# Side-by-side high and low activations in the 256-token feed-forwards of a two-block transformer kernel

## Chip, cores and metric

One core of one Trainium2 chip runs the whole program. The metric is the device time of one execution in microseconds (us). The kernel's text names the engines `tensor` (TensorE, PE in the profile), `vector` (VectorE, DVE), `scalar` (ScalarE, ACT), `gpsimd` (GpSimd, POOL) and `sync` (SyncE, SP, which only starts transfers).

## The reference, cut to what matters

Four transformer layers of width 1024 run over 256 tokens; the first of them also carries 256 context tokens, so its matrices meet 512 tokens. Layers 1 and 2 have one feed-forward each, layers 3 and 4 have two each. That makes six feed-forwards, of which five see 256 tokens:

```python
D_FF = 2816
def swiglu(h, w_in, w_out):            # first two layers; swiglu_2 is the same with silu(g) * u
    a, u = jnp.split(h @ w_in, 2, axis=-1)
    return (jax.nn.silu(a) * u) @ w_out
# layer 2:        x = x + g2 * swiglu(modulate(rms_norm(x, norm2), sh2, sc2), w_ffn_in, w_ffn_out)
# layers 3 and 4: x = x + 0.5 * swiglu_2(rmsnorm(x, g), w_gu, w_down)   before and after the mixer
```

## The kernel before

**Layout.** Features lie on the 128 partitions, tokens along the free dimension (`S` = 256, `SQ` = 512). The 1024 features are 8 chunks (`KC`), the 2816 hidden features 22 tiles (`FT`).

**Products.** A product in full precision is made of three matmuls of float32r parts. Weights and activations are each split into a high part (a rounding copy) and a low part (the value less its high part); `product` (line 873) adds high x high, high weight x low activation and low weight x high activation into one PSUM tile. So each output tile takes three weight loads and three matmuls of 256 columns for each of its chunks. PSUM tiles of these products take three banks in turn (`LIN`), and a tile waits in `room` until the tile three before it has been read.

**Weights.** A "piece" is one transfer into a ring of four slots. ScalarE copies its two halves to `w_hi` (line 1205), of which there are two; VectorE subtracts, half by half, into `ring_lo` (line 1608), in the same place as the piece. Both do this in `ahead`, at the head of their work for an item: at item i they split the piece of item i+1, and ScalarE may begin once TensorE has begun item i's own piece (line 1202), since only then the other `w_hi` is free.

**A feed-forward** (`ffn`, line 659) has 22 `gate_up` items and 8 `resid` items; each engine goes through the items in this one order. A `gate_up` item has one piece of 2048 columns (gate and up weights of one hidden tile): TensorE makes the gate tile a and then the up tile u, 24 matmuls each. In the feed-forwards of layers 3 and 4 ("scaled") the norm's factor `row` is applied behind the product. The order on the other engines at item i is

- ScalarE: split of the next piece; `hid_part` (line 1303, high part of the hidden tile i-1); silu of a (line 1315 if scaled, else line 1318 straight from PSUM).
- VectorE: split of the next piece; `hid_rest` (line 1730, low part of the hidden tile i-1); if scaled, a times `row` out of PSUM (line 1743); the multiply of silu(a) by u (line 1750).
- GpSimd: nothing.

The buffers `tmp` (in `prob_t`) alternate, 512 wide each, of which 256 are in use here. A `resid` item has two pieces of 1408 columns, 11 hidden tiles each, and one output tile; VectorE adds it to the residual (lines 1772 and 1774 if scaled, line 1780 else), ScalarE makes the next stage's high part and a square (lines 1218 and 1222), GpSimd adds the squares (line 1499), VectorE makes the low part (line 1787). Output tile 0 goes chunk by chunk through the three matmuls, waiting for each hidden tile in turn; the others take all matmuls with the high weights of a piece first and those with the low weights last.

Of the kernel before, what the change touches and what calls it, by code (L numbers as in the profile page):

```python
# [122 lines left out]
class Fill:  # L123


    def __init__(self, bank, room, full, taken):
        self.bank, self.room, self.full, self.taken = bank, room, full, taken

# [52 lines left out]
def hybrid_kernel(nc, xt, vec_d, con_d, tables_d, rpb, w, out):  # L181

    with ExitStack() as ctx:  # L183
# [11 lines left out]
        h_hi = sb("h_hi", KC * SQ, F32R)  # L195
        l_at = nc.sbuf_base
        h_lo = sb("h_lo", KC * SQ, F32R)
# [24 lines left out]
        hid_hi, hid_lo = over("hid_hi", FT * S, a_at), over("hid_lo", FT * S, a_at + 4 * FT * S)  # L222
# [17 lines left out]
        gate_lo = over("gates_b", KC * S, h_at + 4 * KC * S, F32)  # L240
        gate_hi = over("gates_c", KC * S, l_at + 4 * KC * S, F32)
# [32 lines left out]
        def plain(a):  # L274
            return a.bitcast(F32)

        def v(name, at=0, n=1):
            return vec[:, VEC[name] + at:VEC[name] + at + n]
# [17 lines left out]
        silu_done, hid_hi_ready, hid_ready = sem("silu_done"), sem("hidden_hi_ready"), sem("hidden_ready")  # L296
        two_in, two_out, gains_ready = sem("two_norms_in"), sem("two_norms_out"), sem("gains_ready")
# [112 lines left out]
        def gate_up(src, i, T, fresh=None, norm=None, scaled=False):  # L410
# [4 lines left out]
            u = linear()  # L415
            if norm:
                norm.update(spread(**norm["of"]))
            add("gate_up", p=p, i=i, T=T, a=a, u=u, fresh=fresh, norm=norm, n=count("hid"), late=i > 0, scaled=scaled,
                silu=count("silu") if scaled else None, prev=last_u[0])
            last_u[0] = u  # L420

        def resid(srcs, tiles, T, how, parts, g=None, nxt=None):

            pieces, tiles = [piece(s, n) for s, n in srcs], [(c, linear()) for c in tiles]
            xd = [count("x_done") if how == "half" else None for _ in tiles]
# [58 lines left out]
        def first_block(l):  # L484
# [152 lines left out]
            for u in range(4):  # L637
                resid([(w["wo"][l][u], SLOT)], (2 * u, 2 * u + 1), T, "mod",
                      [[(0, (k * 2 + m) * P, k) for k in range(KC)] for m in range(2)], (l, 16), ("stats",))
                plan.items[-1].update(src=(h_hi, h_lo, SQ, "mg", plan.counts["mg"] - KC))  # L640
# [7 lines left out]
            for half in range(2):  # L648
# [5 lines left out]
                for c in range(KC):  # L654
                    resid([(down[2 * c + half], 11 * P)], (c,), T, "mod", [[(0, k * P, k) for k in range(11)]], (l, 40),
                          ("stats",) if half else None)
                    plan.items[-1].update(src=(hid_hi, hid_lo, T, "hid", plan.counts["hid"] - FT // 2))

        def ffn(w_in, w_out, how, g, nxt, fresh=None, norm=None):
# [5 lines left out]
            for c in range(KC):  # L665
                resid([(w_out[2 * c + k], 11 * P) for k in range(2)], (c,), S, how,
                      [[(k // 11, (k % 11) * P, k) for k in range(FT)]], g, nxt)
                plan.items[-1].update(src=(hid_hi, hid_lo, S, "hid", plan.counts["hid"] - FT))
# [4 lines left out]
        def second_block(l):  # L673
# [140 lines left out]
            for u in range(4):  # L814
                resid([(w["out2"][l][u], SLOT)], (2 * u, 2 * u + 1), S, "plain",
                      [[(0, (k * 2 + m) * P, k) for k in range(KC)] for m in range(2)], None, ("defer", v("g_ffn2", 8 * l, 8)))
                plan.items[-1].update(src=(mg2_hi, mg2_lo, S, "mg", plan.counts["mg"] - KC))
# [36 lines left out]
        def _(pe):  # L854
# [18 lines left out]
            def product(fs, n, groups, fresh=None, need=None):  # L873
# [5 lines left out]
                left = [3 * sum(len(terms) for _, terms in groups)] * len(fs)  # L879
# [1255 lines left out]
```

## Time and profile before

| what | value |
|---|---|
| time, median of 3 runs | 2614.39 us (2610.23 to 2614.93) |
| span of the profiled execution, first to last instruction | 2610.7 us |
| TensorE busy | 2504.7 us, 96% |
| VectorE busy | 1348.3 us, 52% |
| ScalarE busy | 1147.7 us, 44% |
| GpSimd busy | 343.9 us, 13% |
| granted TensorE clock, mean | 0.986 |

The profile gives the span of its execution; what the device time holds beyond it is not shown, and the span lies 3.7 us under the median. Busy shares are averages over the whole program. In the timelines a row is an instruction, or several alike merged with their count; the bracket behind it is how long the engine had been idle and what ended that.

### The profile page before, as it was taken

The page shows a single profiled execution, that of the slowest core. Times are in us where ns is not written, and L with a number is a line of the kernel's source. Part 1 is how long each engine was busy: PE and PEld are TensorE (multiplying, and loading weights), DVE is VectorE, ACT ScalarE, POOL GpSimd, SP SyncE. Part 2 cuts the span into 40 slices and gives each one's busy share as a digit, 9 for nine tenths or more (in the row PEclk, how much of TensorE's full clock was granted, in tenths as well). Part 3 has the DMA queues.
Part 4 walks back from the last instruction along what each step waited for, and adds up shares of the span by engine and source line. Part 5 has one row for each costly group of instructions (what it writes and reads, how often), then busy time and mean ns, then how long its engine had stood idle before and what let it go on. Part 6 is the DMA issues. An engine that isn't in the chain of part 4 may idle for free. (4 is left out here: it accounts for less than half of the span.)

```text
span 2610.7 us, 40864 instructions
## 1 busy us (share of the span) xinstructions
PE 2504.7 (96%) x17090; PEld 2211.8 (85%) x17090; DVE 1348.3 (52%) x2303; ACT 1147.7 (44%) x1966; POOL 343.9 (13%) x340
## 2 busy tenths in 40 slices
PE   6998999999999999999999999989999999998998
PEld 3754778677777877899999998989999998898998
DVE  2235335433323535655566567556556566656554
ACT  4243443422222525554454444555445444445443
POOL 1233312000001205200000000230000000023000
PEclk9998999999999999999999999999999999999999
DMA  8523123353443322345455443345455454334544
GB/s 295 211 72 111 65 81 129 132 177 122 147 163 131 138 81 82 130 160 180 167 210 185 170 168 118 132 151 179 169 188 193 163 188 148 126 116 167 179 169 139
DMA packets 70424, 393.43 MB, mean 151 GB/s; under 512 B 6688, under 2 KB 6848, under 8 KB 39904
## 3 DMA queue, kind: packets, MB, share of 16 engines
q1 hardware_dynamic: 60864, 350.89, 39.0%
q0 software_dynamic: 9376, 39.91, 4.3%
q8 instruction: 136, 2.23, 0.3%
q14 instruction: 48, 0.39, 0.1%
HBM read 389.73 MB, written 1.05 MB: 150 GB/s over the span
## 5 line engine op out<-in xcount | busy, mean ns | idle before, releaser
L897 PE MATMUL ps<-h_hi,w_hi 128*128 128x256 f32 (+1 forms) x3424 | 957.7, 311 | 15.4 <-ACT h_hi L1253 13.7
L1608 DVE TENSOR_TENSOR ring_lo<-ring,w_hi 128x1024 fp32r<-128x1024 f32 (+3 forms) x712 | 770.8, 1124 | 378.1 <-ACT w_hi L1205 377.9
L897 PE MATMUL ps<-h_lo,w_hi 128*128 128x256 f32 (+1 forms) x3424 | 942.6, 307 | 0.0
L1205 ACT ACTIVATE w_hi<-ring 128x1024 fp32r<-128x1024 f32 (+3 forms) x712 | 642.9, 951 | 459.1 <-PE ps L897 415.8
L897 PEld LDWEIGHTS ps<-h_hi,w_hi 128*128 128x128 f32 x3424 | 654.8, 192 | 71.6 <-issue 42.4
L897 PEld LDWEIGHTS ps<-h_lo,w_hi 128*128 128x128 f32 x3424 | 655.0, 192 | 28.4
L897 PE MATMUL ps<-h_hi,ring_lo 128*128 128x256 f32 (+1 forms) x3424 | 573.2, 306 | 0.0
L897 PEld LDWEIGHTS ps<-h_hi,ring_lo 128*128 128x128 f32 x3424 | 490.5, 192 | 28.8
L897 PE MATMUL ps<-hid_hi,w_hi 128*128 128x256 f32 (+1 forms) x1056 | 287.6, 301 | 0.0
L897 PE MATMUL ps<-hid_lo,w_hi 128*128 128x256 f32 (+1 forms) x1056 | 287.2, 301 | 0.0
L1533 POOL TENSOR_SCALAR logits<-logits,stat 128x512 f32<-128x512 f32 (+2 forms) x140 | 161.4, 1166 | 614.9 <-DVE stat L1856 614.9
L1750 DVE TENSOR_TENSOR prob_t<-prob_t,ps 128x256 f32<-128x256 f32 (+1 forms) x132 | 61.5, 466 | 309.0 <-issue 279.0
L1499 POOL TENSOR_TENSOR logits<-logits 128x256 f32<-128x256 f32 (+1 forms) x77 | 72.5, 941 | 1087.5 <-ACT logits L1222 895.8
L897 PEld LDWEIGHTS ps<-hid_hi,w_hi 128*128 128x128 f32 x1056 | 202.0, 191 | 8.5 <-issue 1.7
L897 PEld LDWEIGHTS ps<-hid_lo,w_hi 128*128 128x128 f32 x1056 | 202.0, 191 | 6.9
L897 PE MATMUL ps<-hid_hi,ring_lo 128*128 128x256 f32 (+1 forms) x1056 | 180.7, 301 | 0.0
L1357 ACT ACTIVATE logits<-logits,stat 128x512 f32<-128x512 f32 (+2 forms) x140 | 81.5, 583 | 186.9 <-DVE logits L1844 87.6
L897 PEld LDWEIGHTS ps<-hid_hi,ring_lo 128*128 128x128 f32 x1056 | 151.6, 191 | 6.8
L1315 ACT ACTIVATE prob_t<-prob_t 128x256 f32<-128x256 f32 x88 | 36.7, 418 | 161.5 <-DVE prob_t L1743 161.5
L1222 ACT ACTIVATE logits<-x_res 128x256 f32<-128x256 f32 (+1 forms) x88 | 40.8, 466 | 124.1 <-DVE x_res L1780 85.0
L897 PE MATMUL ps<-y_lo,w_hi 128*128 128x256 f32 (+1 forms) x272 | 77.6, 307 | 0.0
L1780 DVE SCALAR_TENSOR_TENSOR x_res<-ps,mod,x_res 128x256 f32<-128x256 f32 x64 | 28.6, 480 | 93.5 <-PE ps L897 93.5
(240 smaller groups left out, 2280.4 us busy)
## 6 DMA issues: line engine op xcount, KB each, us to landing
ring<-w_ffn_in SPq DMA_DIRECT2D x132, 1024.0 KB, 4.9
ring<-w_ffn_out SPq DMA_DIRECT2D x96, 704.0 KB, 4.1
ring<-w_in SPq DMA_DIRECT2D x42, 1024.0 KB, 4.9
ring<-w_w_in SPq DMA_DIRECT2D x30, 1024.0 KB, 4.9
bias_t<-w_mod POOLq DMA_DIRECT2D x24, 1024.0 KB, 8.1
ring<-w_mod SPq DMA_DIRECT2D x16, 1024.0 KB, 6.0
ring<-w_up SPq DMA_DIRECT2D x16, 576.0 KB, 3.7
ring<-w_pab SPq DMA_DIRECT2D x8, 1024.0 KB, 4.8
```

The costliest lines, as they stand in the source:

```text
L897: mm = pe.matmul(ps[fs[k].bank][:, 0:n], (hi_w if wpart == "hi" else lo_w)[0:rows, at[k]:at[k] + P], hi if part == "hi" else lo, start=lef ...
L1205: act.activation(w_hi[q.s % 2][:, h * n:(h + 1) * n], ring[q.slot][:, h * n:(h + 1) * n], ACT.Copy)\
L1222: act.activation(by_s(dst, T), xt_of(c, T), ACT.Square).then_inc(squares, 1)
L1315: act.activation(t, t, ACT.Silu).then_inc(silu_done, 1)
L1357: act.activation(lg, lg, ACT.Exp, scale=-1.0, bias=stat[:, o:o + 1], accum_out=stat[:, 4 + o:5 + o])\
L1499: pool.tensor_tensor(sq_sum[:, 0:n], sq_sum[:, 0:n], sq[c % 2][:, 0:n], ALU.add).then_inc(sq_added, 1)
L1533: pool.tensor_scalar(lg, lg, stat[:, 8 + (a % 2) * 2 + h:9 + (a % 2) * 2 + h], None, ALU.mult)\
L1608: dve.tensor_tensor(ring_lo[q.slot][:, c], ring[q.slot][:, c], plain(w_hi[q.s % 2][:, c]), ALU.subtract)\
L1750: dve.tensor_tensor(tmp[2 + i % 2][:, 0:T], t, ps[u.bank][:, 0:T], ALU.mult).then_inc(psum_taken[u.bank], 1)
L1780: ins = dve.scalar_tensor_tensor(xs(c, s), ps[f.bank][:, s * S:(s + 1) * S], mod[l][:, o:o + 1], xs(c, s), ALU.mult, ALU.add)
```

## The change

In the feed-forwards of 256 tokens the high and low parts of the activations lie side by side, 512 columns wide (`h_all`, `hid_all`). The high weights meet both in one matmul of 512 columns ("both"), whose two halves of a PSUM bank then hold the product with the high and with the low part; the low weights meet the high part in one matmul of 256, added to the first half. So a chunk takes two weight loads and two matmuls in place of three. The two halves have to be added:

- `gate_up`: VectorE takes all 512 columns of a out of PSUM (times `row`, or a plain copy in layer 2), GpSimd adds the halves, ScalarE takes silu in SBUF. VectorE multiplies the 512 columns of u by silu(a) used twice, GpSimd adds the halves, and only then can `hid_part` begin.
- `resid`: VectorE adds the halves to the residual in two instructions, with a wait for the first between them.

In products by chunk, the first chunk takes "both" first; the others take the low weights first. All else, the 512-token layer too, keeps its order.

```diff
@@ product (TensorE)
-                left = [3 * sum(len(terms) for _, terms in groups)] * len(fs)
+                two = fs[0].two
+                left = [(2 if two else 3) * sum(len(terms) for _, terms in groups)] * len(fs)
...
+                    if two and by_chunk:
+                        order = [(*parts, t, k) for i, t in enumerate(terms)
+                                 for parts in ((("lo", "hi"), ("hi", "both")) if i or left[0] < first else (("hi", "both"), ("lo", "hi")))
+                                 for k in range(len(fs))]
+                    elif two:
+                        order = [("hi", "both", t, 0) for t in terms] + [("lo", "hi", t, 0) for t in terms]
@@ ScalarE
-            def hid_part(u, i, T):
-                taken(u)
-                act.activation(at_T(hid_hi, i, T), tmp[2 + i % 2][:, 0:T], ACT.Copy).then_inc(hid_hi_ready, 1)
+            def hid_part(g, i, T):
+                if g["u"].two:
+                    act.wait_ge(halves_summed, g["summed"])
+                else:
+                    taken(g["u"])
+                act.activation(hid_part_of(0, i, T), tmp[2 + i % 2][:, 0:T], ACT.Copy).then_inc(hid_hi_ready, 1)
...
-                if st["scaled"]:
-                    taken(st["a"])
+                if st["a"].two:
+                    act.wait_ge(halves_summed, st["summed"] - 1)
                     act.activation(t, t, ACT.Silu).then_inc(silu_done, 1)
@@ GpSimd
+            def pool_gate_up(st):
+                i = st["i"]
+                for f, t in ((st["a"], tmp[i % 2]), (st["u"], tmp[2 + i % 2])):
+                    if f.two:
+                        taken(f)
+                        pool.tensor_tensor(t[:, 0:S], t[:, 0:S], t[:, S:SQ], ALU.add).then_inc(halves_summed, 1)
@@ VectorE, gate_up
-                if st["scaled"]:
+                if a.two:
                     full(a)
-                    dve.tensor_tensor(t, ps[a.bank][:, 0:T], row[:, 0:T], ALU.mult).then_inc(psum_taken[a.bank], 1)
+                    if st["scaled"]:
+                        ins = dve.tensor_tensor(by_s(tmp[i % 2], SQ), by_s(ps[a.bank], SQ), on_both(row[:, 0:S]), ALU.mult)
+                    else:
+                        ins = dve.tensor_copy(tmp[i % 2], ps[a.bank][:, 0:SQ])
+                    ins.then_inc(psum_taken[a.bank], 1)
                     dve.wait_ge(silu_done, st["silu"])
...
-                dve.tensor_tensor(tmp[2 + i % 2][:, 0:T], t, ps[u.bank][:, 0:T], ALU.mult).then_inc(psum_taken[u.bank], 1)
+                if u.two:
+                    dve.tensor_tensor(by_s(tmp[2 + i % 2], SQ), on_both(t), by_s(ps[u.bank], SQ), ALU.mult).then_inc(psum_taken[u.bank], 1)
@@ VectorE, resid
+                def first_half(ins):
+                    halves[0] += 1
+                    ins.then_inc(x_first, 1)
+                    dve.wait_ge(x_first, halves[0])
...
-                        t = tmp[c % 4][:, 0:S]
-                        dve.tensor_tensor(t, ps[f.bank][:, 0:S], row[:, 0:S], ALU.mult).then_inc(psum_taken[f.bank], 1)
+                        t = tmp[c % 4]
+                        dve.tensor_tensor(by_s(t, SQ), by_s(ps[f.bank], SQ), on_both(row[:, 0:S]), ALU.mult).then_inc(psum_taken[f.bank], 1)
                         taken(f)
-                        dve.scalar_tensor_tensor(xs(c, 0), t, 0.5, xs(c, 0), ALU.mult, ALU.add).then_inc(x_done, 1)
+                        first_half(dve.scalar_tensor_tensor(xs(c, 0), t[:, 0:S], 0.5, xs(c, 0), ALU.mult, ALU.add))
+                        dve.scalar_tensor_tensor(xs(c, 0), t[:, S:SQ], 0.5, xs(c, 0), ALU.mult, ALU.add).then_inc(x_done, 1)
                         continue
+                    elif f.two:
+                        l, g = st["g"]
+                        by = mod[l][:, 2 * (g + c):2 * (g + c) + 1]
+                        first_half(dve.scalar_tensor_tensor(xs(c, 0), ps[f.bank][:, 0:S], by, xs(c, 0), ALU.mult, ALU.add))
+                        ins = dve.scalar_tensor_tensor(xs(c, 0), ps[f.bank][:, S:SQ], by, xs(c, 0), ALU.mult, ALU.add)
```

## Rows read from the trace of the kernel before

**Rows 1.** Chain that ended last, in order of time: start, length, what

```profile
2416.45 184.33 PE ps L897 x1536
```

**Rows 2.** Timeline of TensorE in a gate_up item of 256 tokens (start, us, engine, what)

```profile
2449.89 1.12 PE L897 MATMUL ps<-h_hi,ring_lo 128*128 128x256 f32 x8
2450.85 0.28 PE L897 MATMUL ps<-h_hi,w_hi 128*128 128x256 f32 x1
```

**Rows 3.** Timeline of ScalarE and VectorE in a gate_up item of 256 tokens

```profile
2451.23 2.01 ACT L1205 ACTIVATE w_hi<-ring 128x1024 fp32r<-128x1024 f32 x2 [1.18 <-PE ps L897]
2452.33 2.36 DVE L1608 TENSOR_TENSOR ring_lo<-ring,w_hi 128x1024 fp32r<-128x1024 f32 x2 [0.80 <-ACT w_hi L1205]
...
2454.61 0.42 DVE L1730 TENSOR_TENSOR hid_lo<-prob_t,hid_hi 128x256 fp32r<-128x256 f32 x1
2454.94 0.42 DVE L1743 TENSOR_TENSOR prob_t<-ps,row 128x256 f32<-128x256 f32 x1
2455.39 0.42 ACT L1315 ACTIVATE prob_t<-prob_t 128x256 f32<-128x256 f32 x1 [1.84 <-DVE prob_t L1743]
2456.87 0.42 DVE L1750 TENSOR_TENSOR prob_t<-prob_t,ps 128x256 f32<-128x256 f32 x1 [1.51 <-issue]
```

**Rows 4.** Timeline of TensorE in a resid item of 512 tokens

```profile
810.51 2.66 PE L897 MATMUL ps<-hid_hi,ring_lo 128*128 128x512 f32 x11
813.00 0.39 PE L897 MATMUL ps<-hid_hi,w_hi 128*128 128x512 f32 x1
```

**Rows 5.** Groups by form: instructions, shapes, count, busy us and mean ns, idle before

```profile
L897 PE MATMUL ps<-h_hi,ring_lo 128*128 128x256 f32 x2704 | 389.3, 283 | 0.0
...
L897 PE MATMUL ps<-hid_hi,w_hi 128*128 128x256 f32 x880 | 218.9, 283 | 0.0
...
L1750 DVE TENSOR_TENSOR prob_t<-prob_t,ps 128x512 f32<-128x512 f32 x22 | 15.1, 688 | 142.4 <-issue 121.0 <-PE ps L897 20.4 <-ACT prob_t L1318 1.0
```

**Rows 6.** Timeline of the mixer's merge: VectorE hands a tile to GpSimd

```profile
2364.24 0.42 DVE L1917 TENSOR_TENSOR prob_t<-ps,gates_b 128x256 f32<-128x256 f32 x1
...
2364.80 0.74 POOL L1548 TENSOR_TENSOR prob_t<-prob_t 128x256 f32<-128x256 f32 x1 [2.27 <-DVE prob_t L1917]
```

**Rows 7.** Timeline of the merge: a split beside a GpSimd add

```profile
2350.65 1.43 DVE L1608 TENSOR_TENSOR ring_lo<-ring,w_hi 128x576 fp32r<-128x576 f32 x2 [0.69 <-ACT w_hi L1205]
...
2353.13 2.00 DVE L1608 TENSOR_TENSOR ring_lo<-ring,w_hi 128x576 fp32r<-128x576 f32 x2
...
2353.45 1.07 POOL L1551 TENSOR_TENSOR prob_t<-prob_t 128x256 f32<-128x256 f32 x1
...
2354.55 0.42 ACT L1416 ACTIVATE mg_hi<-prob_t 128x256 fp32r<-128x256 f32 x1 [0.37 <-POOL prob_t L1551]
```

**Rows 8.** Timeline of a scaled resid item, from the next output tile's first matmul on

```profile
1458.04 0.28 PE L897 MATMUL ps<-hid_hi,w_hi 128*128 128x256 f32 x1
...
1458.24 0.42 DVE L1772 TENSOR_TENSOR prob_t<-ps,row 128x256 f32<-128x256 f32 x1 [1.26 <-PE ps L897]
...
1458.70 0.43 DVE L1774 SCALAR_TENSOR_TENSOR x_res<-prob_t,x_res 128x256 f32<-128x256 f32 x1
...
1459.88 1.46 ACT L1205 ACTIVATE w_hi<-ring 128x704 fp32r<-128x704 f32 x2
...
1460.69 1.69 DVE L1608 TENSOR_TENSOR ring_lo<-ring,w_hi 128x704 fp32r<-128x704 f32 x2 [0.50 <-ACT w_hi L1205]
```

**Rows 9.** Timeline of layer 2's resid items: another split beside an add

```profile
1274.96 1.30 POOL L1499 TENSOR_TENSOR logits<-logits 128x512 f32<-128x512 f32 x1 [151.23 <-ACT logits L1224]
1275.60 1.41 DVE L1608 TENSOR_TENSOR ring_lo<-ring,w_hi 128x704 fp32r<-128x704 f32 x1 [0.90 <-ACT w_hi L1205]
```

**Rows 10.** Timeline of the last feed-forward where gate_up item 1 begins

```profile
2416.21 0.37 PE L897 MATMUL ps<-h_hi,w_hi 128*128 128x256 f32 x1
...
2416.95 0.42 DVE L1743 TENSOR_TENSOR prob_t<-ps,row 128x256 f32<-128x256 f32 x1
```

**Rows 11.** Timeline of VectorE at the start of layer 3's first feed-forward

```profile
1331.05 3.25 DVE L1759 SCALAR_TENSOR_TENSOR x_res<-x_res,vec,row 128x256 f32<-128x256 f32 x8
```

More of the change, by code:

```diff
@@ L127, in __init__ @@
         self.bank, self.room, self.full, self.taken = bank, room, full, taken
+        self.two = False
 class Piece:
@@ L415, in gate_up @@
             u = linear()
+            a.two = u.two = T == S
             if norm:
@@ L418, in gate_up, with resid @@
             add("gate_up", p=p, i=i, T=T, a=a, u=u, fresh=fresh, norm=norm, n=count("hid"), late=i > 0, scaled=scaled,
-                silu=count("silu") if scaled else None, prev=last_u[0])
-            last_u[0] = u
-        def resid(srcs, tiles, T, how, parts, g=None, nxt=None):
+                silu=count("silu") if T == S else None, summed=count("summed", 2) if T == S else None, prev=last_u[0])
+            last_u[0] = plan.items[-1]
+        def resid(srcs, tiles, T, how, parts, g=None, nxt=None, two=False):
             pieces, tiles = [piece(s, n) for s, n in srcs], [(c, linear()) for c in tiles]
+            for _, f in tiles:
+                f.two = two
             xd = [count("x_done") if how == "half" else None for _ in tiles]
@@ L888, in product @@
                         pe.wait_ge(w_hi_ready, 2 * p.s + 2)
-                    for wpart, part, (at, hi, lo, rows, c), k in order:
+                    for wpart, part, (at, rows_of, rows, c), k in order:
                         if wpart == "lo" and p.n not in lo_seen:
@@ L892, in product @@
                             pe.wait_ge(w_lo_ready, 2 * p.s + 2)
[L893 to L895 removed]
+                        if fresh is not None and k == 0:
+                            if part == "both" or wpart == part:
+                                pe.wait_ge(h_hi_ready, fresh - KC + c + 1)
+                            if part != "hi":
+                                pe.wait_ge(h_lo_ready, fresh - KC + c + 1)
+                            if two and wpart == "lo":
+                                pe.wait_ge(h_hi_ready, fresh - KC + c + 1)
+                        if need and k == 0 and (two or part == wpart):
                             pe.wait_ge(need[0], need[1] + c + 1)
[L897 to L898 removed]
+                        mm = pe.matmul(ps[fs[k].bank][:, 0:SQ if part == "both" else n],
+                                       (hi_w if wpart == "hi" else lo_w)[0:rows, at[k]:at[k] + P],
+                                       rows_of[part], start=left[k] == first, stop=left[k] == 1)
                         left[k] -= 1
@@ L991, in pe_tok @@
                             c, at = j * per + i, i * cols
-                            for part, wt in ((h_hi, w_hi[p.s % 2]), (h_lo, w_hi[p.s % 2]), (h_hi, ring_lo[p.slot])):
-                                mm = pe.matmul(ps[f.bank][:, 0:st["n"]], at_T(part, c, T, t * P, P), wt[:, at:at + st["n"]],
-                                               start=c == 0 and part is h_hi and wt is w_hi[p.s % 2],
+                            for part, wt in ((0, w_hi[p.s % 2]), (1, w_hi[p.s % 2]), (0, ring_lo[p.slot])):
+                                mm = pe.matmul(ps[f.bank][:, 0:st["n"]], h_part(part, c, T)[:, t * P:(t + 1) * P], wt[:, at:at + st["n"]],
+                                               start=c == 0 and part == 0 and wt is w_hi[p.s % 2],
                                                stop=c == KC - 1 and wt is ring_lo[p.slot])
@@ L1585, in _ @@
         def _(dve):
-            chain, split = [0], [0]
+            chain, split, halves = [0], [0], [0]
             def link(ins):
```

78 lines of the change are left out of this document (47 added, 31 removed).

## The prediction

> **What bounds the kernel now.** I read the chain that ended last first: its longest piece is 1536 matmuls back to back in 184.33 us, 0.120 us each [rows 1]. So in a feed-forward of 256 tokens TensorE waits for nobody. Then the timelines of one `gate_up` item: TensorE starts eight matmuls of 256 columns in 0.96 us [rows 2], so an item of 48 lasts 5.76 us. The other engines do their part in less: if s is the start of silu, the next split starts 0.33 later at the earliest, and from split to silu pass 4.16 us [rows 3], so their round would be 4.49 us; they wait for TensorE (the bracket at the split, and the 1.51 us before the multiply). The slack is 1.27 us per item, and that is what the change spends.
>
> **Part one, TensorE.** Eleven matmuls of 512 start in 2.49 us, 0.2264 each [rows 4]. A chunk took 3 x 0.120 = 0.360 and takes 0.2264 + 0.120 = 0.3464 us: 13.6 ns less. The 256-token feed-forwards have 5 x 22 x 2 x 8 = 1760 such triples in `gate_up` (part of the 2704) and 880 in `resid` [rows 5]: 2640 x 0.0135 = 35.6 us saved if TensorE sets the pace. An item becomes 16 x 0.3464 = 5.54 us, an output tile 22 x 0.3464 = 7.62 instead of 7.92. Bounds where 256 and 512 alternate: nothing (0.240 for 512 columns) to these 13.6 ns; I take the rows, as both rates were measured with a weight load at each matmul.
> The Trainium skill (TensorE: Matmul & The Clock Gate, "Back-to-back issue gap") gives a matmul's spacing as its columns at full clock plus 2.5 ns; by that rule a matmul less would be worth 2.5 and not 13.6 ns. The rows' 120 ns for 256 columns decide against it here.
>
> **Part two, the round of the other engines.** I follow it from silu of item i at s = 0.
> - silu 0.42, hop 0.03 (as from 2455.36 to 2455.39 [rows 3]): the multiply of u starts at 0.45. With 512 columns it takes 0.69 [rows 5]: to 1.14.
> - GpSimd's add starts 0.14 after a VectorE result and takes 0.74 [rows 6]: from 1.28 to 2.02.
> - Meanwhile ScalarE splits the next piece from 0.33 on. VectorE may begin 1.10 after that [rows 3], at 1.43. But its split reads two SBUF operands, like GpSimd's add, and the trace shows such a pair taking turns: two half splits that last 1.43 us alone lasted 2.00 while an add of 0.74 lasted 1.07 [rows 7]; a split of 0.88 (1.69 for two, 0.80 apart, [rows 8]) lasted 1.41 when issued under an add, so it ran from 1276.13, 0.13 before the add's recorded end [rows 9]. GpSimd is first here, by 0.15 us. So the split starts at 2.02 - 0.13 = 1.89.
> - Two halves at 1.14 each, then `hid_rest` 0.33 later [rows 3]: `hid_rest` at 4.17, a out of PSUM from 4.50 to 5.19 (0.69), GpSimd's add from 5.33 to 6.07, the next silu 0.03 behind it (2354.52 to 2354.55 [rows 7]): 6.10.
>
> The round is 6.10 us against 5.54 on TensorE and 5.76 before: two adds with their hops, 0.27 more for the copy of a, 0.27 more for the multiply, 0.46 of waiting for the port. If VectorE's half were first, GpSimd would wait for it, the second half for GpSimd, and the round would be about 6.2.
> The Trainium skill (SBUF — State Buffer, "Who interferes with whom") says that a VectorE instruction with two SBUF inputs and a GpSimd instruction that reads SBUF exclude each other for a whole instruction. The trace agrees but for the 0.13 us of overlap; by the page alone the round would be 6.23 and 100 items some 13 us longer.
>
> **When the round reaches TensorE.** TensorE needs the low weights of item i+2 after its eight matmuls of 512, 1.81 into the item; they are ready at 1.89 + 1.14 + 1.22 + 0.05 = 4.30. So item i+2 starts no earlier than s + 2.5. The bank of the up tile, free at 5.2 and wanted 2.77 into the item, gives 2.45, the same point. In the last feed-forward a of item 0 is read 0.74 after item 1 began [rows 10]; with 0.69 + 0.14 + 0.74 + 0.03 the first silu is at +2.34. Then 19 rounds: 2.34 + 115.9 + 2.5 = 120.7, where TensorE alone would begin item 21 after 20 x 5.54 = 110.9. It stands still for 9.8 us. The same for three feed-forwards: 29.5. In layer 2 a is full as item 1 begins: first silu at 0.1 + 0.69 + 0.91 = 1.7, stall 9.2. At layer 3's start the eight updates of x, 3.25 us on VectorE [rows 11], follow the first multiply; they put the split off from 1.89 to 4.3: stall 12.4 with a first silu at 2.4. Sum 51.1 us.
>
> **The start of `resid`.** Here ScalarE splits piece 23 only after `hid_part` of tile 21, which now waits for silu, the multiply (0.69) and the add. Item 21's round with half splits of 704 columns [rows 8] is 5.29 long, and TensorE, going chunk by chunk, wants the low weights of piece 22 after one matmul: they are 1.3 us late. After that, silu 21 starts 2.0 into output tile 0, its add ends 2.0 later, `hid_part` at 4.1, the split from 4.4, the low weights of both halves at 6.95. TensorE wants them after 11 chunks, at 3.81 (the by-chunk order takes low weights first in piece 23). Stall 3.1. Together 4.4 us, five times: 22.
>
> **Within `resid`.** ScalarE's second split of an output tile begins 1.84 after the tile's first matmul, behind the high part and the square [rows 8], and ends at 3.30; TensorE came for it at 33 x 0.120 = 3.96. The residual is now done 0.27 later for the wider multiply and 0.47 for the second addition with its wait (0.46 from one to the next [rows 8]): the split ends at 4.04, wanted at 3.81. About 0.3 us with the hop, seven tiles in three feed-forwards: 6.3; in layer 2, where only the second addition comes on top, some 0.1, 0.7 in all; none in the last, which makes no high part. The same 0.74 us goes straight to what follows an output tile 7 (three next stages and the program's end), and 0.5 in layer 2: 3.4 us. The adds of squares keep their place behind the square, and DMA rings and hand-over of slots follow TensorE as before.
>
> **Sum.** -35.6 + 51.1 + 22 + 7.0 + 3.4 = +47.9 us: the span of 2610.7 becomes 2658.6. The median lies 3.7 above the profiled span; I keep that: 2662.
>
> **Bounds.** Three operations have no row of their own form: the add of two halves of one buffer (0.74 by [rows 6], at most 1.07 under a split [rows 7]), the multiply with one operand used twice and the copy of a (0.42 as for 256 columns [rows 3] to 0.69 [rows 5], nearest 0.69 as the columns count). 0.05 us in the round is 5 us in the program. With 0.60 for each of the two the round is 5.92 and the total near 2644; with VectorE's half first, 2675. The likeliest case's own range: 2640 to 2685.
>
> **Rivals.**
> - The port costs nothing (POOL and VectorE side by side): round 5.64. Silu then reaches TensorE's limit only at the end: stalls of about 6.5 us in all of `gate_up`, 19 at the starts of `resid`, the rest as above: -35.6 + 6.5 + 19 + 10.4 = +0.3, so 2615. For it: the overlap of 0.13, and that the add at 1.28 and the split at 1.43 are close. Against it: [rows 7, 9]. Chance 0.10, of which 0.07 within 0.2%.
> - TensorE stays the bound: the round fits in 5.54 and the starts of `resid` are covered. That needs a round 0.56 shorter than worked out, more than the port's 0.46; it decides at 5.54. -35.6 + 10.4 = -25: 2589. For it: VectorE is 52% busy, and a wait of mine may be shorter than the rows' hops. Against it: no row shows any term smaller. Chance 0.13; this is the case on the faster side.
> - The matmul of 512 next to 256 saves nothing: in `gate_up` the round sets the pace anyway, in `resid` 11.9 us are lost: 2674. Against it: [rows 2, 4]. Chance 0.06. The Trainium skill's 2.5 ns (same page as above) would leave 2.2 of those 11.9 us and give 2672; I count it with this rival.
> - Longer stalls: the waits at the start of `resid` come on top of a later hidden tile, or the round is VectorE-first and each wait costs a restart of TensorE: 2680 to 2710. Chance 0.06.
>
> The forecast itself has 0.65. This kernel's runs tell 0.2% (5 us) from no change. Faster by more: 0.13. Within: 0.07. Slower: 0.80. The range 2613 to 2692 takes in the no-cost port, the idle saving and most of the longer stalls, and leaves out the faster case and what is above, under 2 in 10.
>
> **What would show it.** Right: TensorE's gate_up items 5.54 us apart at first, then some 6.1; silu to silu 6.1 in every feed-forward of 256 tokens; splits on VectorE 2.36 + about 0.45 for a pair; the half split no longer released by TensorE but by ScalarE's own order; PE's idle time put down to `ring_lo` or PSUM, some 80 us in all; a hole of about 3 us before piece 23; matmul pitch 0.226 and 0.120. Wrong: pairs of splits still at 2.36 beside the add (first rival); silu to silu at 5.54 with ScalarE waiting for TensorE (second); matmul pitches other than these. The forecast fails most easily by the slack being larger than 2.5 lets it, since 20 rounds add up any error.

## The result, and the profile after

The changed kernel takes 2662.7 us (median of 4 runs, 2660.6 to 2666.4), the kernel before 2612.6 in the same series: ratio 1.0192, 95% interval 1.0180 to 1.0204, slower. The profiled execution has a span of 2657.5 us against 2610.7, 46.8 us more. The page of the profile after: engines, then the chain that ended last, by engine.

```profile
PE 2512.2 (95%) x14450; PEld 2078.3 (78%) x14450; DVE 1484.9 (56%) x2365; ACT 1138.2 (43%) x1966; POOL 508.9 (19%) x560
...
PE 4%; DVE 3%; ACT 1%; POOL 1%; issue 1%; POOLq 0%; DVEq 0%
```

PE is still busy for 95% of the time, with 2640 matmuls fewer. What changed is the last line: the long piece of matmuls of [rows 1] is gone, and VectorE, ScalarE and GpSimd now stand in the chain.

One item of `gate_up` in the last feed-forward, and ahead of it the pair of splits of the item before (start, us, engine, what; rows left out at the dots). Lines of the changed file: L933 `product`, L1250 and L1663 the splits, L1351 and L1785 high and low part of the hidden tile, L1363 silu, L1799 a times `row`, L1810 the multiply of u, L1554 GpSimd's two adds.

```profile
2494.24 2.78 DVE L1663 TENSOR_TENSOR ring_lo<-ring,w_hi 128x1024 fp32r<-128x1024 f32 x2 [0.26 <-ACT w_hi L1250]
...
2498.80 0.42 ACT L1363 ACTIVATE prob_t<-prob_t 128x256 f32<-128x256 f32 x1 [3.34 <-POOL prob_t L1554]
...
2499.15 2.01 ACT L1250 ACTIVATE w_hi<-ring 128x1024 fp32r<-128x1024 f32 x2
2499.25 0.69 DVE L1810 TENSOR_TENSOR prob_t<-prob_t,ps 128x512 f32<-128x512 f32 x1 [1.30 <-ACT prob_t L1363]
...
2500.02 0.74 POOL L1554 TENSOR_TENSOR prob_t<-prob_t 128x256 f32<-128x256 f32 x1 [1.25 <-DVE prob_t L1810]
2500.24 2.74 DVE L1663 TENSOR_TENSOR ring_lo<-ring,w_hi 128x1024 fp32r<-128x1024 f32 x2 [0.30 <-ACT w_hi L1250]
...
2501.30 2.08 PE L933 MATMUL ps<-h_all,w_hi 128*128 128x512 f32 x8 [0.19 <-ACT w_hi L1250]
...
2502.91 0.41 DVE L1785 TENSOR_TENSOR hid_all<-prob_t,hid_all 128x256 fp32r<-128x256 f32 x1
...
2503.24 0.68 DVE L1799 TENSOR_TENSOR prob_t<-ps,row 128x512 f32<-128x512 f32 x1
2503.99 0.74 POOL L1554 TENSOR_TENSOR prob_t<-prob_t 128x256 f32<-128x256 f32 x1 [3.23 <-DVE prob_t L1799]
...
2504.77 0.42 ACT L1363 ACTIVATE prob_t<-prob_t 128x256 f32<-128x256 f32 x1 [3.31 <-POOL prob_t L1554]
```

From silu to silu pass 5.97 us here, and 5.95 to 5.97, mostly 5.96, in all rounds but the first ones and the last of a feed-forward. The pair of half splits takes 2.78 us beside the add (first line; the item shown, with 2.74, is an exception), and took 2.36 before [rows 3]. In [rows 3] ScalarE's split was released by TensorE; now it follows silu, silu waits for GpSimd, and TensorE waits for the split: the new item starts at 2501.30, 2.50 after silu, and the bracket names `w_hi`.

The span by stretches, as sums over the five feed-forwards of 256 tokens, read off the matmuls' starts: `gate_up` is from item 1 to the first matmul of `resid`, `resid` from there to the next stage's first matmul (in the last feed-forward to its own last matmul), the rest is all else. In layer 2 the last two high-weight matmuls of item 0 stand directly ahead of item 1 and are counted with it, 0.2 us before and 0.5 after.

| us | before | after | difference |
|---|---|---|---|
| gate_up | 605.4 (121.0 to 121.2 each) | 621.1 (123.3 to 126.8) | +15.7 |
| resid | 316.7 (63.4 each) | 342.3 (67.0 to 69.7) | +25.6 |
| rest | 1688.6 | 1694.1 | +5.5 |

The rest varies from profile to profile: in the runs below it was 1688.8 to 1697.6, and what precedes the first of these feed-forwards alone 1135.6 to 1140.5. Part of that is the clock: by the mean granted clocks TensorE was at the lower clock, outside the stretches of the table, for some 74 us in the profile before, 80 in the changed kernel's, and 64 in that of e10 below. The two other rows repeat within about 1 us where the clock does.

The start of `resid` in the last feed-forward, where most of the second row comes from (rows left out at the dots):

```profile
2577.43 2.23 DVE L1663 TENSOR_TENSOR ring_lo<-ring,w_hi 128x704 fp32r<-128x704 f32 x2
...
2577.52 1.40 POOL L1554 TENSOR_TENSOR prob_t<-prob_t 128x256 f32<-128x256 f32 x1 [1.25 <-DVE prob_t L1810]
...
2579.72 0.51 PE L933 MATMUL ps<-hid_all,ring_lo 128*128 128x256 f32 x2 [0.87 <-DVE ring_lo L1663]
...
2581.45 0.42 ACT L1363 ACTIVATE prob_t<-prob_t 128x256 f32<-128x256 f32 x1 [2.08 <-POOL prob_t L1554]
...
2583.44 0.42 ACT L1351 ACTIVATE hid_all<-prob_t 128x256 fp32r<-128x256 f32 x1 [1.57 <-POOL prob_t L1554]
...
2583.76 1.45 ACT L1250 ACTIVATE w_hi<-ring 128x704 fp32r<-128x704 f32 x2
...
2584.57 1.69 DVE L1663 TENSOR_TENSOR ring_lo<-ring,w_hi 128x704 fp32r<-128x704 f32 x2 [0.26 <-ACT w_hi L1250]
...
2586.36 0.36 PE L933 MATMUL ps<-hid_all,ring_lo 128*128 128x256 f32 x1 [2.72 <-issue]
```

TensorE waits 0.87 us for the low weights of the first piece and 2.72 for those of the second: silu, multiply, add, high part, split and subtraction of the last hidden tile stand in line ahead of them. The bracket of the wait of 2.72 names no releaser; that it is for these weights is read from the subtraction, which ends at 2586.26, and tested below by an earlier split. In the first two lines VectorE's split was first by 0.09 us, and there the add of 0.74 took 1.40: whoever comes second waits.

Then the clock, by windows in the same feed-forward (bounds and length, busy time of each engine, granted clock, DMA share, GB/s):

```profile
2583.30:2586.30 3.00, 0.35 (x2) 0.03 (x1) 2.12 (x3) 1.77 (x3) 0.11 (x1) 1.00 0.00 0
2587.30:2590.70 3.40, 3.40 (x13) 2.88 (x12) 1.69 (x2) 0.99 (x2) 0.00 (x0) 0.52 0.66 212
2591.00:2600.00 9.00, 9.00 (x53) 7.86 (x52) 5.20 (x8) 3.25 (x5) 0.00 (x0) 1.00 0.50 162
```

Behind the hole, for 3.4 us, the granted clock is 0.52, which is the lower of the two levels (1.2 GHz against 2.4) but for a small part: 13 matmuls in place of some 20. It is so in four of the five feed-forwards, not in the fourth. The prediction has nothing of this.

### The profile page after: what moved, and what is told of

Same layout as the page of the kernel before. It is cut to its first block and busy times, and to the rows that moved or that the text cites. A ratio compares the mean times of both kernels' runs of the same rounds, so it can differ in the third digit from the quotient of the medians.

```text
span 2657.5 us, 35915 instructions
## 1 busy us (share of the span) xinstructions
PE 2512.2 (95%) x14450; PEld 2078.3 (78%) x14450; DVE 1484.9 (56%) x2365; ACT 1138.2 (43%) x1966; POOL 508.9 (19%) x560
## 3 DMA queue, kind: packets, MB, share of 16 engines
HBM read 389.73 MB, written 1.05 MB: 147 GB/s over the span
## 5 line engine op out<-in xcount | busy, mean ns | idle before, releaser
L933 PE MATMUL ps<-h_all,w_hi 128*128 128x512 f32 (+1 forms) x5088 | 1069.2, 357 | 27.5 <-ACT h_all L1298 11.5
L1663 DVE TENSOR_TENSOR ring_lo<-ring,w_hi 128x1024 fp32r<-128x1024 f32 (+3 forms) x712 | 814.5, 1185 | 307.3 <-ACT w_hi L1250 307.0
L933 PEld LDWEIGHTS ps<-h_all,w_hi 128*128 128x128 f32 x5088 | 823.3, 190 | 183.1 <-issue 69.5
L1250 ACT ACTIVATE w_hi<-ring 128x1024 fp32r<-128x1024 f32 (+3 forms) x712 | 641.2, 948 | 300.7 <-PE ps L933 257.8
L933 PE MATMUL ps<-h_all,ring_lo 128*128 128x256 f32 (+1 forms) x3424 | 570.5, 306 | 1.9 <-DVE ring_lo L1663 1.9
L933 PEld LDWEIGHTS ps<-h_all,ring_lo 128*128 128x128 f32 x3424 | 500.1, 191 | 53.2 <-DVE ring_lo L1663 2.3
L933 PE MATMUL ps<-hid_all,w_hi 128*128 128x512 f32 x1232 | 321.3, 398 | 1.8
L933 PEld LDWEIGHTS ps<-hid_all,w_hi 128*128 128x128 f32 x1232 | 229.4, 190 | 54.4 <-ACT w_hi L1250 6.1
L1554 POOL TENSOR_TENSOR prob_t<-prob_t 128x256 f32<-128x256 f32 x220 | 165.9, 754 | 508.4 <-DVE prob_t L1799 291.0
L933 PE MATMUL ps<-hid_all,ring_lo 128*128 128x256 f32 (+1 forms) x1056 | 182.7, 303 | 18.0 <-issue 13.7
L1363 ACT ACTIVATE prob_t<-prob_t 128x256 f32<-128x256 f32 x110 | 46.0, 418 | 358.8 <-POOL prob_t L1554 358.8
L933 PEld LDWEIGHTS ps<-hid_all,ring_lo 128*128 128x128 f32 x1056 | 158.0, 193 | 33.4 <-issue 15.1
L1810 DVE TENSOR_TENSOR prob_t<-prob_t,ps 128x512 f32<-128x512 f32 x110 | 75.7, 688 | 142.9 <-ACT prob_t L1363 142.9
L1812 DVE TENSOR_TENSOR prob_t<-prob_t,ps 128x512 f32<-128x512 f32 x22 | 15.1, 688 | 142.4 <-issue 121.0
L933 PE MATMUL ps<-y_lo,w_hi 128*128 128x256 f32 (+1 forms) x272 | 77.6, 308 | 0.0
L1080 PE MATMUL ps<-arena 64*128 64x512 f32 (+2 forms) x280 | 68.1, 525 | 5.2 <-DVE logits L1918 4.3
```

The costliest lines, as they stand in the source:

```text
L933: mm = pe.matmul(ps[fs[k].bank][:, 0:SQ if part == "both" else n], (hi_w if wpart == "hi" else lo_w)[0:rows, at[k]:at[k] + P], rows_of[par ...
L1080: pe.matmul(ps[f.bank][:, 0:sp_["nk"]], p["q"][a, t * P:(t + 1) * P], p["k"][a, 0:sp_["nk"]], start=True, stop=True).then_inc(psum_full[f. ...
L1250: act.activation(w_hi[q.s % 2][:, h * n:(h + 1) * n], ring[q.slot][:, h * n:(h + 1) * n], ACT.Copy)\
L1363: act.activation(t, t, ACT.Silu).then_inc(silu_done, 1)
L1554: pool.tensor_tensor(t[:, 0:S], t[:, 0:S], t[:, S:SQ], ALU.add).then_inc(halves_summed, 1)
L1663: dve.tensor_tensor(ring_lo[q.slot][:, c], ring[q.slot][:, c], plain(w_hi[q.s % 2][:, c]), ALU.subtract)\
```

## The experiments

All times are medians of the runs, ratios are to the kernel before in the same series (2611.9 us in that of e1 to e4, 2612.8 in that of e5 to e8, 2614.6 in that of e9 to e12), and come from all its runs, so they differ slightly from the quotient of the medians. "Stretches" are those of the table.

**One add less, or the same time without the port (three runs).** The first leaves out the add of u's halves, so the hidden tile lacks the product with the low part; the second leaves out that of a; the third puts a write of GpSimd's of the same length, which reads nothing, in place of the add of u.

```diff
-                for f, t in ((st["a"], tmp[i % 2]), (st["u"], tmp[2 + i % 2])):
+                for f, t in ((st["a"], tmp[i % 2]),):                     # e1; e2 keeps u alone
...
+                            pool.memset(bias_t[:, 8 * S:11 * S], 0.0).then_inc(halves_summed, 1)   # e3, for u
```

> Leaves out GpSimd's add of the two halves of u (the product of the up weights with the low activations is missing in the hidden tiles); hid_part follows VectorE's multiply. u's add is not itself a link from silu to silu; it can touch that round only by holding up VectorE's split. Theory (the round of the other engines sets the pace, 0.38 of its 5.96 us is the split waiting for this add): round 5.96 - 0.38 = 5.58, just under TensorE's 5.59, so the gate_up stretches fall from 123.7 to about 117.4 us (some 31 us in five feed-forwards), and the wait at the start of resid shrinks by at least the add's 0.8 us: about 2616 us in all, 2610 to 2625. Rival (the add and the split do not hinder each other, the round is long for other reasons): items stay at 5.96, only the starts of resid gain 0.8 us each, 2648 to 2658 us.

> Leaves out GpSimd's add of the two halves of a (silu sees the gate weights' product with the high activations alone); silu follows VectorE's instruction. Theory: this add and its hop (0.74 + 0.07 us) are a link of the round, so the round is 5.96 - 0.8 = 5.15 us and TensorE (5.59 us per item) sets the pace again: gate_up stretches of about 117.4 us, splits still lengthened by u's add (2.74 in place of 2.36 us for a pair), about 2620 us, 2612 to 2628. Rival (TensorE's own spacing or the weight split alone sets 5.96): items stay at 5.96 and the time at 2655 to 2663 us.

> In place of u's add GpSimd writes zeros to 768 columns of a scratch buffer (it reads nothing; the low part of u is missing in the hidden tiles); by the 0.31 us of the 256-column memset in the trace against 0.10 for one column it should last about as long as the add, 0.7 us. All waits and the order stay. Theory (the port is held by an instruction that reads SBUF on GpSimd beside one with two SBUF inputs on VectorE): the pair of splits is back at 2.36 us, round 5.58, gate_up stretches near 117.4, the starts of resid as before: about 2630 us, 2622 to 2638. Rival A (any GpSimd instruction holds VectorE up): pairs of 2.74, 2660 us. Rival B (no port, GpSimd's time alone counts): 2655 to 2663 us too, but with pairs of 2.36.

| | time | ratio | round while TensorE does not hold it | pair of splits | gate_up | resid |
|---|---|---|---|---|---|---|
| e1 | 2606.1 | 0.9982 (0.9973 to 0.9992) | 5.55 | 2.36 | 589.5 | 319.6 |
| e2 | 2604.9 | 0.9969 (0.9959 to 0.9980) | 5.15 | 2.78 in these rounds, then 2.39 | 588.8 | 320.2 |
| e3 | 2609.8 | 0.9991 (0.9982 to 1.0000) | 5.55 | 2.36 | 589.5 | 323.6 |

The timeline of the third, GpSimd and VectorE side by side:

```profile
2439.12 0.74 POOL L1555 MEMSET bias_t<- 128x768 f32 x1 [1.23 <-DVE prob_t L1813]
...
2439.33 2.36 DVE L1666 TENSOR_TENSOR ring_lo<-ring,w_hi 128x1024 fp32r<-128x1024 f32 x2 [0.26 <-ACT w_hi L1250]
```

A write that keeps GpSimd busy for the same 0.74 us leaves the pair at 2.36; the add makes it 2.78. So it is GpSimd's reading of SBUF beside a split with two SBUF operands that costs, about 0.4 us a round, and neither GpSimd's time nor the later high part: the round is 5.55 with the write and without anything. It is enough to go under TensorE's own 5.59, and `gate_up` falls to 117.4 to 117.8 us in four stretches, about 3.5 less than before (layer 3's first takes 118.8 to 119.5). In e2 the add of u is still there. In the first rounds of a feed-forward the pair takes 2.78 as in the changed kernel, and the round is 5.15 all the same, shorter by the add of a and its hand-over. From the point where TensorE sets the pace ScalarE's split waits for TensorE; only the first 0.18 us of VectorE's then lie beside the add, and the pair takes 2.39. The Trainium skill (SBUF — State Buffer, "Who interferes with whom") has this rule, two SBUF inputs on VectorE against a GpSimd instruction that reads SBUF and not against one that only writes; these runs agree, with 2.78 and 2.36.

The times came out some 10 to 20 us lower than I expected. I had left the starts of `resid` nearly as long as in the changed kernel. But where TensorE sets the pace in `gate_up`, the others reach the last item early: the wait for the first piece is gone, that for the second is down from 2.9 us to between nothing and 2.4, and no stretch had the lower clock behind it.

**The start of resid: an earlier split.** ScalarE and VectorE split the second piece before they treat the last hidden tile.

```diff
             def act_hidden(st):
+                if "first" in st:
+                    ahead(st["first"])
...
             def dve_hidden(st):
+                if "first" in st:
+                    ahead(st["first"])
```

> Computes all. In the item between gate_up and resid, ScalarE and VectorE split the second resid piece before they make the last hidden tile's high and low parts; nothing else moves. Theory (the 2.7 us hole in output tile 0 is that split queued behind the add of u, and the half clock after it follows from the hole): the split starts 2.0 us earlier, the hole falls to under 1 us, and the slow 3.4 us after it (512 columns every 0.43 us) are gone in the four feed-forwards that have them, 1.6 us each: 5 x 2.0 + 4 x 1.6 = 16 us, 2646 us. If the slow stretch has another cause, 2652 us. Rival (the hole is the wait for a hidden tile and not for the weights): no change, 2662 us or more. gate_up items stay at 5.96 us in every case.

Measured 2646.9 us, ratio 1.0134 (1.0119 to 1.0149); `gate_up` 621.0 as in the changed kernel, `resid` 328.8: 3 us less in four stretches and 1.4 in the fourth. The wait is 1.4 us shorter, where 2.0 were expected; the other 1.6 are the lower clock, which no stretch shows now and the fourth did not have in the changed kernel's profile.

**Each half of the change alone.** The one run takes the new form out of `gate_up` (with the old lines for a, u and silu), the other out of `resid` (with the old two lines for the residual).

```diff
-            a.two = u.two = T == S                    # e5
...
-                      [[(k // 11, (k % 11) * P, k) for k in range(FT)]], g, nxt, two=True)
+                      [[(k // 11, (k % 11) * P, k) for k in range(FT)]], g, nxt)      # e6
```

> Only the resid items keep the change; gate_up goes back to three matmuls of 256 and GpSimd does nothing there. Theory: this half of the change is worth about nothing. Five resid stretches lose 10 us on TensorE (2.0 each), three of them give back 0.37 in each of seven tiles behind the later split (7.8 us), and the second addition adds about 3 us at the ends of the stretches. The 25.6 us that the resid stretches lengthened came from the adds of gate_up, so they are gone here: stretches of 61.5 to 64.5, gate_up 121.0 as before, 2615 us (2607 to 2622). Rival: the lengthening of the resid stretches came from the change of resid itself (the second addition and its wait); then stretches stay at 67 to 69.6 and the time is 2637 to 2645.

> Only the gate_up items keep the change; resid goes back to three matmuls of 256 and one addition. Theory: nearly the whole loss is here. gate_up 123.3 to 126.8 as in the changed kernel (+15.7 us in all), the resid stretches 63.4 plus a start hole of about 4 to 5.5 with the half clock behind it (+20 to +27), little else: 2653 us (2645 to 2661). Rival as above: the holes belong to the two-matmul order of resid; then the stretches are back at 63.4 to 65 and the time is 2628 to 2636.

Measured: e5 2620.1 us, ratio 1.0026 (1.0016 to 1.0037), gate_up 605.5, resid 315.9 (62.4, 64.0 to 64.2 scaled, 61.3 in the last). e6 2651.7 us, ratio 1.0147 (1.0132 to 1.0162), gate_up 621.3, resid 337.6 (67.2 to 68.6). The loss is in `gate_up`'s half, and the holes at the start of `resid` come with it though `resid` itself is as before: 1.25, 1.75 and 1.05 us from one matmul to the next in every stretch. Only the last of the five had the lower clock behind them. The resid half saves 2.0 us a stretch on TensorE and gives most of it back inside, 0.8 us are left in the five. That e5 is slower all the same has its cause outside the stretches: the rest is 8.9 us longer in its profile. Of these, 4.5 go in the four transitions behind `resid` and at the end of the program, where the second addition comes ahead of all that follows (see below); the other 4.4 lie in the parts that vary.

**No GpSimd: VectorE sums the halves.** A reduction over the pair reads 512 columns of PSUM and writes 256.

```diff
+            def sum_of(t, f):
+                dve.tensor_reduce(t, ps[f.bank][:, :].rearrange("p (s t) -> p t s", s=2), AX_X, ALU.add)\
+                    .then_inc(psum_taken[f.bank], 1)
...
+                    sum_of(t, a)
+                    if st["scaled"]:
+                        taken(a)
+                        dve.tensor_tensor(t, t, row[:, 0:S], ALU.mult).then_inc(halves_summed, 1)
...
+                    sum_of(h, u)
+                    taken(u)
+                    dve.wait_ge(silu_done, st["silu"])
+                    dve.tensor_tensor(h, t, h, ALU.mult).then_inc(halves_summed, 1)
```

> Computes everything. Matmuls as in the changed kernel, but in gate_up VectorE sums the two halves of a bank itself, straight from PSUM (one reduction over the pair, 512 columns in and 256 out, at about 0.69 us by its columns), then multiplies by the row, and sums u while ScalarE takes silu; GpSimd does nothing in gate_up. Theory: no hand-over to GpSimd, no shared port, silu's time hidden behind the sum of u: a round of about 5.2 us, under TensorE's 5.59. gate_up 117.4 to 119.5 (-16 us in all), resid stretches 62.5 to 65 as where one add was left out, no half clock: 2604 us (2597 to 2612). Rival: the reduction reads its pairs across the bank and costs twice the columns (1.2 us or more): then the round is 6.2 and the time 2670 or above; or VectorE's added work costs what GpSimd's did: 2650 to 2665.

e8 adds the earlier split of e4 and, in the scaled `resid` items:

```diff
-                        dve.tensor_tensor(by_s(t, SQ), by_s(ps[f.bank], SQ), on_both(row[:, 0:S]), ALU.mult).then_inc(psum_taken[f.bank], 1)
+                        sum_of(t[:, 0:S], f)
                         taken(f)
-                        first_half(dve.scalar_tensor_tensor(xs(c, 0), t[:, 0:S], 0.5, xs(c, 0), ALU.mult, ALU.add))
-                        dve.scalar_tensor_tensor(xs(c, 0), t[:, S:SQ], 0.5, xs(c, 0), ALU.mult, ALU.add).then_inc(x_done, 1)
+                        first_half(dve.tensor_tensor(t[:, 0:S], t[:, 0:S], row[:, 0:S], ALU.mult))
+                        dve.scalar_tensor_tensor(xs(c, 0), t[:, 0:S], 0.5, xs(c, 0), ALU.mult, ALU.add).then_inc(x_done, 1)
```

> Computes everything. As the one before, and in the scaled resid items VectorE also sums the halves in one reduction, multiplies by the row and adds once; and the second piece of resid is split before the last hidden tile. Theory: gate_up 117.4 to 119.5, the holes at the start of resid close (they are about 1 us where TensorE sets the pace), the 0.37 us in each later tile stays since the residual takes as long as before: resid stretches 62 to 64.5, 2599 us (2590 to 2606), faster than the kernel before. Rival: the reduction costs twice, then 2665 or above; or the order of the split gains nothing once the round is short: 2604, as the run before.

Measured: e7 2605.4 us, ratio 0.9964 (0.9952 to 0.9976), gate_up 588.7, resid 318.1. e8 2600.3 us, ratio 0.9950 (0.9935 to 0.9964), gate_up 588.7, resid 315.8. VectorE and ScalarE in e7:

```profile
2442.10 2.36 DVE L1666 TENSOR_TENSOR ring_lo<-ring,w_hi 128x1024 fp32r<-128x1024 f32 x2 [0.23 <-ACT w_hi L1250]
...
2444.71 0.69 DVE L1792 TENSOR_REDUCE prob_t<-ps 128x256 f32<-128x512 f32 x1
2445.43 0.42 DVE L1808 TENSOR_TENSOR prob_t<-prob_t,row 128x256 f32<-128x256 f32 x1
2445.89 0.42 ACT L1366 ACTIVATE prob_t<-prob_t 128x256 f32<-128x256 f32 x1 [2.57 <-DVE prob_t L1808]
```

The reduction costs what its columns say, 0.69 us. The round is 5.19 until it meets TensorE's 5.59. VectorE is busier than in the changed kernel (59% against 56%) and the time is 57 us shorter: its share was not what cost, the hand-overs and the port were.

**Inside resid: the split ahead of the high part.** A scaled tile of the changed kernel, ScalarE and TensorE:

```profile
1954.53 0.51 ACT L1263 ACTIVATE h_all<-x_res,vec 128x256 fp32r<-128x256 f32 x1 [3.73 <-DVE x_res L1843]
1954.94 0.40 ACT L1267 ACTIVATE logits<-x_res 128x256 f32<-128x256 f32 x1
...
1955.25 1.46 ACT L1250 ACTIVATE w_hi<-ring 128x704 fp32r<-128x704 f32 x2
...
1956.76 2.81 PE L933 MATMUL ps<-hid_all,w_hi 128*128 128x512 f32 x11
```

ScalarE was idle for 3.73 us, then the high part, the square and the split follow each other, and TensorE starts as the split ends.

```diff
             def act_resid(st):
                 for p in st["pieces"]:
                     ahead(p)
+                if "then" in st:
+                    ahead(st["then"])        # first piece of the next output tile
```

> Computes everything. As the run before with VectorE's sums, and in resid ScalarE splits the first piece of the next output tile before it makes this tile's high part and square. Theory: what costs 0.37 to 0.41 us in each later output tile of the scaled resid stretches (8.04 to 8.08 instead of 7.67) is the split that stands behind high part and square on ScalarE, and those come later since the residual is done later; with the split ahead of them the tiles go to 7.67. 21 tiles at 0.4 and seven at 0.15: 9.5 us off 2600.3, so 2591 us (2587 to 2596). Rival: the tiles wait for the residual itself (the bank of PSUM or VectorE's own split behind it), then the order on ScalarE changes nothing: 2600.

> Only the resid items side by side, gate_up in three matmuls, plus the order of the run before (ScalarE splits the next output tile's first piece ahead of this tile's high part). Theory: 2620.1 less 9.5 = 2611 us (2606 to 2615), about the kernel before less what the resid stretches save on TensorE, plus the later end of each stretch. Rival, as above: 2620. If the order gave nothing here and did in the run before, the cause would lie in VectorE's load.

Measured: e9 2595.4 us, ratio 0.9924 (0.9911 to 0.9937), and e10 2605.6 us, ratio 0.9973 (0.9961 to 0.9984). In both every tile falls to 7.67 and the stretches to 61.4, 306.9 and 307.1 in sum, 8.9 and 8.8 less than without the order. e9 lies some 4 us above the point I gave and e10 some 5 below; the resid stretches are as expected, and by the profiles the remainder is in the rest of the program (1697.6 and 1691.1), which scatters, in part by the clock. Of e9:

```profile
1912.94 1.47 ACT L1255 ACTIVATE w_hi<-ring 128x704 fp32r<-128x704 f32 x2 [2.36 <-PE ps L938]
...
1914.32 0.50 ACT L1268 ACTIVATE h_all<-x_res,vec 128x256 fp32r<-128x256 f32 x1
...
1916.28 2.68 PE L938 MATMUL ps<-hid_all,w_hi 128*128 128x512 f32 x11
```

The split is done 1.9 us before TensorE comes for it.

**The hole filled.** TensorE runs 12 matmuls into an unused bank while it would stand still.

```diff
+                    if two and need and left[0] < first:
+                        for _ in range(12):
+                            pe.matmul(ps[7][:, 0:SQ], prev_w[:, 0:P], both_of(hid_all, 0), start=True, stop=True)
```

> The changed kernel, and in the 3.1 us in which TensorE stands still before the second piece of resid it runs 12 matmuls of 512 columns into an unused bank (2.7 us). All results are as before; nothing waits for these matmuls. Theory: the 3.4 us of half clock behind that hole follow TensorE's standing still; with the hole filled the granted clock stays at 1.00 there, and four stretches lose 1.6 us each: 2662.7 - 6.4 = 2656 us (2652 to 2660). Rival: the clock falls for what comes after (another load, the transfers), and the time stays at 2662; or the added matmuls end after the low weights are there and add up to 0.3 us each.

> The changed kernel once more, unchanged, for one profile. If the half clock behind the hole of 3.1 us belongs to the kernel's own course, it shows in the same four of five stretches (not in the fourth); if it depends on when the chip looks, other stretches show it. Time 2661 to 2666 either way.

Measured: e11 2656.4 us, ratio 1.0160 (1.0146 to 1.0173), against 1.0192 for the changed kernel; resid 336.3 against 342.3. Windows of e11 over the hole and behind it:

```profile
2581.00:2584.20 3.20, 3.18 (x16) 2.31 (x14) 2.12 (x3) 1.78 (x3) 0.22 (x1) 1.00 0.00 0
2584.20:2592.00 7.80, 7.80 (x45) 6.88 (x46) 4.18 (x7) 3.25 (x5) 0.00 (x0) 1.00 0.58 184
```

The clock stays at 1.00 in all five stretches, with the same work behind the hole. So the lower clock follows the standing still, and it costs 6.0 us over four stretches, 1.5 each. The changed kernel once more (one run, 2664.5 us) had it in all five, in the last one for longer (resid 68.1 instead of 67.0): which stretch is hit, and for how long, changes from run to run, and that the fourth was spared in the first profile was chance. The Trainium skill (TensorE: Matmul & The Clock Gate, "What's actually happening") says that a TensorE left idle falls back to the lower clock; the granted clock here, 0.52 behind the hole and 1.00 with the hole filled, agrees.

## Why the prediction was right

The sign, the mechanism and the size were as forecast: 2662.7 against 2662, span 2657.5 against 2658.6. That it comes so close is luck: `gate_up` as a whole gained 15.7 us where 27.4 were forecast, `resid` 25.6 where 17.1 were, the rest 5.5 where 3.4 were, and these errors cancel.

- **TensorE.** Forecast: items of 5.54, tiles of 7.62. Measured where nothing holds it: 5.59 and 7.67 (117.4 us over 21 items, e7; 61.4 over eight tiles, e9). The rates of [rows 2] and [rows 4] hold nearly: a chunk takes 0.349 us and not 0.346, as matmuls of 512 start 0.231 apart in e7 and not 0.226. So 18 us are saved in `gate_up`, where 23.7 were forecast, and 10 in `resid`, forecast 11.9. The rival that the pair saves nothing falls. The 2.5 ns that the prediction quotes are given in the Trainium skill (TensorE: Matmul & The Clock Gate, "Back-to-back issue gap") for an isolated matmul. With a weight load for each, as here, a matmul of 256 starts every 0.120 us, 13 ns more than its columns take at 2.4 GHz.
- **The round.** Forecast 6.10, measured 5.96. Splits beside the add, `hid_rest`, a out of PSUM all came as written; the two hand-overs from VectorE to GpSimd took 0.08 and 0.07 us and not the 0.14 of [rows 6] (2499.25 + 0.69 = 2499.94, the add at 2500.02), and that is all of the difference. The operations without a row of their own (add, multiply with a repeated operand, product or copy of a) took 0.74, 0.69 and 0.68, the values that the sum used. e1 and e3 show the port directly; the rival that it costs nothing falls, and so does the one in which TensorE stays the bound, which is reached only where one add or the price of the port is taken away (e1 to e3).
- **Where the round meets TensorE.** Forecast: the next item starts 2.5 after silu; measured 2.50. I named the low weights and the bank of u; the profile names the high weights, whose split also follows silu.
- **Stalls in gate_up.** Forecast 51.1 us, measured 33.7 (621.1 less 587.4, which is five stretches at TensorE's pace): 0.14 us less in 20 rounds of five feed-forwards is 14 us, as the prediction warned. TensorE's own item, 0.05 longer in 21 items of five, is 5 more that are no stall but TensorE's. This term was forecast too large.
- **Starts of resid.** Forecast 4.4 each, 22 in all. The two holes, 1.25 and 3.12 us from one matmul's start to the next, cost 1.0 + 2.9 = 3.9 over the matmuls' own spacing (4.1 in the whole last stretch of e11, 65.4 against 61.3), 20 in all. The lower clock behind them, 6 us, was in no term.
- **Within resid.** Forecast 0.3 a tile in three feed-forwards and 0.1 in layer 2, 7.0 us. Measured with the hole filled (e11): 68.1 less 65.4 = 2.7 in each scaled stretch, 0.39 a tile, and 1.2 in layer 2, together 9.5. e9 and e10 show the cause: the split behind the high part. So `resid` as a whole gained 25.6 where 17.1 was forecast.
- **Transitions and end.** Forecast 3.4: 0.5 behind layer 2's `resid` and 0.74 at each of four other places. Measured in the profiles: from the next stage's first matmul to its first with `ones`, which waits for GpSimd's sum of squares, 3.43 us become 3.93 behind layer 2, and 2.88 become 3.59 or 3.60 at the three others; at the end, from the last matmul of `resid`, 2.57 become 3.29. So this term came as forecast; the run without the change in `resid` (e6) has the old numbers at all five. One of the three (6.66 to 7.29 in all) gains 0.1 back. The end takes 1.8 in all (10.3 to 12.1), of which 1.1 was in no term. Of that, 0.8 is the clock: the last matmuls run at the lower level (granted 0.54 from 2648.7 to 2651.4, against 0.96 before in the same place), and their two groups take 0.86 and 1.22 us in place of 0.61 and 0.71.

Of the +5.5 in the rest, 4.4 have a place by this; the other 1.1 lie within the scatter of the unchanged parts. Open is what decides which hole is followed by the lower clock.

## What to carry to other kernels

A matmul fewer per chunk paid about 11 ns each here (0.17 us in an item of 16 chunks), and it shortens the time in which everything else must be done: add up the whole round of the other engines, hand-overs and port included, before trusting that TensorE stays the bound. Here the change became a gain (0.9924) by summing the halves on the engine that takes them out of PSUM anyway, which removes two hand-overs and the port, and by putting what TensorE waits for ahead of what nobody waits for. A wait of about 3 us on TensorE has to be priced with the clock behind it, here 1.5 us each time.

## What the runs showed of the hardware

- A GpSimd write of 0.74 us beside a VectorE subtraction of two SBUF operands costs nothing (2.36 us a pair, e3); a GpSimd add of 0.74 us costs 0.42 (2.78), and 0.66 the other way round where VectorE is first (1.40 for the add). In the first order the split, reckoned back from its end with its length alone, starts about 0.14 us before the add's recorded end (2500.24 + 2.74 - 2.36 = 2500.62 against 2500.02 + 0.74 = 2500.76).
- VectorE to GpSimd takes 0.07 to 0.08 us here, about half of what [rows 6] show.
- TensorE at the lower clock after standing still: holes of 1.25 and 3.12 us were followed by it in nine of ten stretches of the two profiles of the changed kernel, holes of 1.25 and 1.67 to 1.73 in none of five (e4), 1.25, 1.75 and 1.05 in one of five (e6), and a single hole of 2.62 not in its one case (e3). Filling 2.9 of the 3.1 us removed it in all five (e11).
- A reduction over pairs that lie 256 columns apart in a PSUM bank runs at the pace of its 512 input columns, 0.69 us.
